# Pooled projections of the token mixer: three rounded passes through the weight ring, most of them early, in place of full-precision products

## The reference, cut to what matters

```python
def token_mixer(h, mix_w_in, conv_w, ..., pool_w, pool_scale, pool_proj, dn_proj, mix_w_out):
    proj = h @ mix_w_in
    xp, q, k, v, z, b_raw, a_raw, g_pool, g_dn = jnp.split(proj, MIX_IN_SPLITS, axis=-1)

    pooled = multiscale_pool(xp)
    ya = jnp.einsum('btgc,gcd->btgd', pooled, pool_w).reshape(B, T, POOL_WIDTH) * pool_scale
    ya = ya @ pool_proj

    qkv = jax.nn.silu(causal_depthwise_conv(jnp.concatenate([q, k, v], axis=-1), conv_w))
    ...
    merged = jax.nn.sigmoid(g_pool) * ya + jax.nn.sigmoid(g_dn) * yb
    return merged @ mix_w_out
```

## Time and profile before

| | |
|---|---|
| runs, median (lowest to highest) | 1830.85 us (1830.83 to 1831.58), 3 runs |
| the profiled execution, first to last instruction | 1829.4 us |
| TensorE busy | 1804.5 us of it |
| mixer, heads of k, q and v | some 985 to 1240 us of the span |

### The profile page before, as it was taken

The page is one execution under the profiler, slowest core; times in us unless marked ns, Lnnn a source line. Parts: engine busy times, 40 slices in busy tenths (PEclk is TensorE's granted clock), DMA queues, the critical chain, the costliest instruction groups (busy, mean ns, idle before and its releaser), DMA issues.

```text
span 1829.4 us, 22015 instructions
## 1 busy us (share of the span) xinstructions
PE 1804.5 (99%) x8636; PEld 1442.0 (79%) x8636; DVE 1090.7 (60%) x1927; ACT 842.3 (46%) x1371; POOL 141.0 (8%) x159
## 2 busy tenths in 40 slices
PE   8999999999999999999999999999999999999998
PEld 6777777767888788888886877788888878888887
DVE  6787888877526887633348777745434763333323
ACT  5777777777423422322225766335422443222221
POOL 2200000000011022100100120100000100000010
PEclk9999999999999999999999999999999999999999
DMA  5422332322243498623323222310222422222231
GB/s 192 138 104 81 116 104 73 113 93 100 73 173 137 163 322 294 212 90 97 100 84 144 78 85 91 104 59 12 81 92 89 153 85 100 95 101 90 95 97 65
DMA packets 59478, 209.21 MB, mean 114 GB/s; under 512 B 6704, under 2 KB 9136, under 8 KB 58736
## 3 DMA queue, kind: packets, MB, share of 16 engines
q1 hardware_dynamic: 47248, 164.54, 26.0%
q0 software_dynamic: 12128, 43.26, 7.1%
HBM read 202.53 MB, written 5.25 MB: 114 GB/s over the span
## 4 chain that ended last, share of the span: by engine, by line
PE 91%; DVE 5%; ACT 2%; issue 1%; DMA 0%; SPq 0%; DVEq 0%; ACTq 0%
PE ps L1335 25%; PE ps L1338 25%; PE ps L1336 24%; PE ps L1424 2%; PE ps L1448 2%; PE ps L1385 2%; PE ps L1386 2%; PE ps L1477 1%; PE ps L1392 1%; DVE wL L1637 1%; ACT wH L2082 1%; PE ps L1436 1%; PE ps L1413 1%; PE ps L1414 1%; DVE affn L1732 0%
## 5 line engine op out<-in xcount | busy, mean ns | idle before, releaser
L1637 DVE TENSOR_TENSOR wL<-wr,wH 128x1024 fp32r<-128x1024 f32 (+1 forms) x297 | 360.0, 1214 | 368.2 <-ACT wH L2082 367.7
L1335 PE MATMUL ps<-hH,wH 128*128 128x512 f32 (+1 forms) x1448 | 577.6, 399 | 1.0 <-DVE hL L1737 1.0
L1338 PE MATMUL ps<-hH,wL 128*128 128x512 f32 (+1 forms) x1448 | 565.4, 390 | 1.0 <-DVE wL L1637 0.7
L1336 PE MATMUL ps<-hL,wH 128*128 128x512 f32 (+1 forms) x1448 | 563.9, 389 | 0.0
L2082 ACT ACTIVATE wH<-wr 128x1024 fp32r<-128x1024 f32 (+1 forms) x297 | 307.6, 1038 | 238.4 <-PE ps L1338 221.3
L1335 PEld LDWEIGHTS ps<-hH,wH 128*128 128x128 f32 (+1 forms) x1448 | 271.3, 187 | 71.1 <-issue 13.1
L1338 PEld LDWEIGHTS ps<-hH,wL 128*128 128x128 f32 (+1 forms) x1448 | 271.0, 187 | 61.9 <-DVE wL L1637 4.0
L1336 PEld LDWEIGHTS ps<-hL,wH 128*128 128x128 f32 (+1 forms) x1448 | 271.4, 187 | 55.9 <-issue 2.6
L1335 PE MATMUL ps<-gffn,wH 128*128 128x512 f32 (+1 forms) x374 | 142.3, 380 | 0.3 <-DVE xT L1875 0.2
L1338 PE MATMUL ps<-gffn,wL 128*128 128x512 f32 (+1 forms) x374 | 140.9, 377 | 0.0
L1336 PE MATMUL ps<-gffn,wH 128*128 128x512 f32 (+1 forms) x374 | 140.9, 377 | 0.0
(11 more groups left out here) (339 smaller groups left out, 2375.3 us busy)
## 6 DMA issues: line engine op xcount, KB each, us to landing
wr<-wst SPq DMA_DIRECT2D x280, 512.0 KB, 3.4
fed<-wfd POOLq DMA_DIRECT2D x56, 512.0 KB, 5.1
xT<-wfd POOLq DMA_DIRECT2D x16, 512.0 KB, 4.0
wr<-wst SPq DMA_DIRECT2D x16, 384.0 KB, 3.0
xT<-xin SPq DMA_DIRECT2D x8, 256.0 KB, 7.3
xT<-xin SPq DMA_DIRECT2D x2, 1024.0 KB, 5.9
xsave<-xT SPq DMA_DIRECT2D x1, 2048.0 KB, 7.2
c<-wfd POOLq DMA_DIRECT2D x8, 256.0 KB, 3.3
```

Source lines behind the costliest of these rows:

```text
L1335: e.matmul(o, hi, vh, start=k == 0, stop=False)
L1336: e.matmul(o, hi, vl, start=False, stop=False)
L1338: i = e.matmul(o, lo, vh, start=False, stop=k == t.nk - 1)
L1637: e.tensor_tensor(dst, x, hi.bitcast(F32), ALU.subtract).then_inc(s[name], 1)
```

## The change

The f32 products go away. `pool_mid` now gives high and low parts of `ya` (`yH`, `yL`, held in the arena `a3r`): ScalarE writes the scaled high part, and VectorE a new low part. `pool_out(c)` becomes a product tile of kind `po` in the ring: four blocks of 128 (a slot of 128 x 512), 12 rounded matmuls in 4 ticks, ScalarE copies the result to `X`. `pool_gate(c)` is the gate tile, after which VectorE multiplies `X` in place. The first `po` tile stands behind the first group of k, ahead of its session's sums; the other seven stand behind the second group of k, and the sessions of q move by 24 and 20 ticks. The eight f32 weight loads leave GpSimd's queue, and SyncE's queue loads eight more slots. The high part of the squares moves to another place in SBUF (`o3r` for `xr`).

```diff
         def pool_mid(g):
-            add("pool_mid", g=g, bank=wk.take()[1], pm=sig("pm"), ya=sig("ya"), pd=g + 1)
+            add("pool_mid", g=g, bank=wk.take()[1], pm=sig("pm"), ya=sig("ya"), yl=sig("yl"), pd=g + 1)
...
         def pool_out(c):
+
+            po = sig("po")
+            yield from self.steps_of(Tile("po", src("pool_proj_2", 128 * c, 4), pb.take()[1], "y", ("po", po), c=c, po=po))
+
+        def pool_gate(c):
             gps = sig("gps")
-            yield from self.steps_of(tile("gp", 4624 + 128 * c, ("gps", gps), c=c, gps=gps))
-            bank, pp, m1 = pb.take()[1], sig("pp"), sig("m1")
-            for k in range(4):
-                add("pool_out", c=c, k=k, bank=bank, pp=pp, m1=m1, gps=gps)
-                yield k
+            yield from self.steps_of(tile("gp", 4624 + 128 * c, ("gps", gps), c=c, gps=gps, po=c + 1, m1=sig("m1")))
...
         session(32, "k", range(4))
         session(76, "k", range(4, 8))
-        session(120, "q", range(4))
-        session(164, "q", range(4, 8))
+        session(144, "q", range(4))
+        session(184, "q", range(4, 8))
...
-        po = iter(range(8))
         for which in "kq":
             for g in range(2):
                 for h in range(4 * g, 4 * g + 4):
                     run(conv(which, h))
-                run(pool_out(next(po)))
+                run(pool_gate("kq".index(which) * 2 + g))
+                if which == "k":
+                    for c in ((0,), range(1, 8))[g]:
+                        run(pool_out(c))
         for h in range(DNH):
             run(conv("v", h))
             if h % 2:
-                run(pool_out(next(po)))
+                run(pool_gate(4 + h // 2))
...
-                    i = e.matmul(ps[d["bank"]][:], b4(pool_buf[c % 2], k), yab[k], start=k == 0, stop=k == 3)
...
+                elif what == "pool_mid":
+                    g = d["g"]
+                    w.wait_ge(s["ya"], d["ya"])
+                    e.scalar_tensor_tensor(yL[g], ps[d["bank"]][:], S("pool_scale", g, g + 1), yH[g].bitcast(F32),
+                                           ALU.mult, ALU.subtract).then_inc(s["yl"], 1)
+                elif what == "out_gp":
+                    v = X[d["c"]]
+                    w.wait_ge(s["po"], d["po"])
+                    w.wait_ge(s["gps"], d["gps"])
+                    e.scalar_tensor_tensor(v, gpb, 1.0, v, ALU.add, ALU.mult).then_inc(s["m1"], 1)
...
-                    e.activation(yab[g], ps[d["bank"]][:], ACT.Copy, scale=S("pool_scale", g, g + 1)).then_inc(s["ya"], 1)
+                    e.activation(yH[g], ps[d["bank"]][:], ACT.Copy, scale=S("pool_scale", g, g + 1)).then_inc(s["ya"], 1)
+                elif what == "out_po":
+                    t = d["t"]
+                    w.wait_ge(s["slot"], t.done)
+                    w.wait_ge(s["saved"], 16)
+                    e.activation(X[d["c"]], ps[t.bank][:], ACT.Copy).then_inc(s["po"], 1)
```

More of the change, by code:

```diff
@@ L868, in session @@
             for j, h in enumerate(hs):
-                at(end + 13 + j + (2 if end == 164 else 0), l2_sum, h, l2s)
+                at(end + 13 + j + (2 if end == 184 else 0), l2_sum, h, l2s)
                 if which == "k":
@@ L874, in session @@
                     at(end + 38 + 2 * j, prep_q, h)
-            at(end + 17 + (2 if end == 164 else 0), l2, which, l2s)
+            at(end + 17 + (2 if end == 184 else 0), l2, which, l2s)
             at(end + 26, l2_end, which, l2s)
@@ L950, in mixer @@
         head_ends()
-        add("mix_out", om=self.count["om"], pp=8, m1=8)
+        add("mix_out", om=self.count["om"], m1=8)
         def zd_out(h):
@@ L1002, in model_kernel @@
     place, n_main = {}, 0
+    proj_at = {one: 1024 * 9216 + 128 * 128 * 4 + 65536 * c for c, one in enumerate(POOLW[4:])}
     for one in slots:
-        if one not in place:
+        if one not in place and one not in proj_at:
             place[one] = n_main
@@ L1023, in several @@
                 return [self(n) for _ in range(k)]
-        with ExitStack() as early:
-            xR = Arena(early, "xr", 4096, F32R)
         xT = alloc(ctx, "xT", 4096)
@@ L1070, in model_kernel @@
         G = Arena(P1a, "g1a", 3072, F32R)
-        sq3_hi = [xR.t[:, 512 * j:512 * j + 512] for j in range(4, 8)]
         sq_hi, sq_lo = G.several(3), G.several(3)
@@ L1103, in model_kernel @@
             F.close()
+        with ExitStack() as early:
+            o3R = Arena(early, "o3r", 8192, F32R)
+        sq3_hi = [o3R.t[:, 6144 + 512 * j:6656 + 512 * j] for j in range(4)]
         M = ExitStack()
@@ L1120, in model_kernel @@
         sq3_lo = [mR.t[:, 14336 + 512 * j:14848 + 512 * j] for j in range(4)]
+        yH, yL = ([mR.t[:, a + 512 * j:a + 512 + 512 * j] for j in range(4)] for a in (2048, 4096))
         Kdr, rB, vB, gpb = [W[:, 0:512], W[:, 512:1024]], yab[0:2], yab[2:4], C("dist")
@@ L1138, in model_kernel @@
         dsol = nc.dram_tensor("dsol", (4 * 65536,), F32, kind="Internal").ap()
-        rhs = {"h": ([c5(hH, c) for c in range(8)], [c5(hL, c) for c in range(8)]), "g": (gH, gL), "o": (oH, oL), "m": (mH, mL)}
+        rhs = {"h": ([c5(hH, c) for c in range(8)], [c5(hL, c) for c in range(8)]), "g": (gH, gL), "o": (oH, oL), "m": (mH, mL),
+               "y": (yH, yL)}
         g_order = [h for z in range(6) for h in (6 + z, z)] + list(range(12, HEADS))
@@ L1252, in weights @@
                 n = slots[j][2] * slots[j][4]
+                src_d, at = (wfd, proj_at[slots[j]]) if slots[j] in proj_at else (wst, place[slots[j]])
                 e.dma_start(wr[:, (j % NRAW) * SLOT:(j % NRAW) * SLOT + n],
-                            wst[place[slots[j]]:place[slots[j]] + 128 * n].rearrange("(p c) -> p c", p=128)).then_inc(s_raw[j % NRAW], 16)
+                            src_d[at:at + 128 * n].rearrange("(p c) -> p c", p=128)).then_inc(s_raw[j % NRAW], 16)
             for c in range(8):
@@ L1314, in ready @@
                     w.wait_ge(s["ol"], k + 1)
+                elif t.rhs == "y":
+                    w.wait_ge(s["yl"], k + 1)
                 else:
@@ L1937, in _ @@
                     e.tensor_scalar(ngc, gc, -1.0, None, ALU.mult, ALU.bypass).then_inc(s["bd"], 1)
[L1938 to L1941, removed]
-                        w.wait_ge(s["saved"], 16)
-                        e.scalar_tensor_tensor(X[d["c"]], gpb, 1.0, ps[d["bank"]][:], ALU.add, ALU.mult).then_inc(s["m1"], 1)
+                elif what == "pool_mid":
[8 more added lines that the diff above has]
+                    e.scalar_tensor_tensor(v, gpb, 1.0, v, ALU.add, ALU.mult).then_inc(s["m1"], 1)
                 elif what == "conv_taps":
@@ L2405, in pool_feed @@
             def pool_feed():
-                if pool_n[0] < len(POOLW):
+                if pool_n[0] < 4:
                     feed(POOLW, pool_buf, s_pool, pool_n[0], pool_at[0])
-                    pool_at[0] += 128 * POOLW[pool_n[0]][2] * 128
+                    pool_at[0] += 128 * 128
                     pool_n[0] += 1
```

21 lines of the change are left out of this document (4 added, 17 removed).

## The result

| | before | after |
|---|---|---|
| runs, median (lowest to highest) | 1830.84 us (1830.18 to 1831.58), 4 runs | 1841.22 us (1840.40 to 1842.73), 4 runs |
| the profiled execution, first to last instruction | 1829.4 us | 1838.5 us |

The ratio is 1.0057, its 95% interval 1.0046 to 1.0069: the change costs 10.4 us. The forecast was 1835.5 us with a range up to 1839.5, so it was slower, as forecast, and by more than twice as much.

What follows compares the result with a forecast made beforehand. TensorE, busy 1804.5 of 1829.4 us, was taken as the bound. A 5.9 us gain against waits of 3.3, 0.4, 4.6 and 2.3 gave +4.7: 1834.1 profiled, 1835.5 us as median, 8-in-10 range 1831.5 to 1839.5.

Steps and rivals of the forecast that it cites:

- The gain: Eight f32 product groups, 27.5 us, become 96 rounded passes at 0.225 us, 21.6 us: 5.9 us less.
- Place 1: Sums of the first group of k: TensorE waits for VectorE's low part behind copy, gate multiplication and split: +3.3 us.
- The +0.4: Late weight split for the slot behind the first short po tile, in the first group of k: +0.4 us (0 to 0.9).
- Place 2: Sums of the second group of q: more VectorE work before head 7's low part; +4.6 us, a wait of about 5.9.
- Place 3: End of v: without the f32 group TensorE stands until head 7's silu ends, before the transposes: +2.3 us.
- The rival that VectorE has caught up: Seven tiles let VectorE reach q's head 7 early, so no wait there: 1829.6 us, half caught up 1832.5; chance 0.23.
- The sum: Gain and added waits together: -5.9 + 3.3 + 0.4 + 4.6 + 2.3 = +4.7 us.
- the step that took the clock for a rival: Clock falls to 1.2 GHz in the long wait at Place 2, 14 slow passes, 3 us more: 1838.5 us; chance 0.15.
- The rest of the program unchanged within 0.5 us: Sign to check: attention and feed-forward, outside the changed places, stay as they were within 0.5 us.
- The base: Starting time: the profiled 1829.4 us, plus 1.45 us by which the median of the runs lies above it.

Runs made afterwards that it cites:

- the tile of double length: Kernel after the change with 12 unneeded passes in front of each po tile, 96 in all: 1858.56 us.
- all three waits filled: Kernel after the change with passes whose result is overwritten ahead of its three long TensorE waits (12, 22 and 8): 1836.44 us.
- the kernels with filled waits: Kernel after the change with unneeded TensorE passes ahead of Place 2 alone, Places 2 and 3, or all three: 1838.3, 1837.8, 1836.44 us.
- the four kernels that carry unneeded passes: Kernel after the change with passes ahead of one, two or three waits, or before each po tile: 1838.3, 1837.8, 1836.44, 1858.56 us.
- the version with the gate tiles moved: Kernel after the change, gate multiplication 6 ticks later, no gate tile behind k's second group, two at the end, q's last sums 3 ticks later: 1831.16 us.

## Why the prediction was wrong

**The gain, -5.9 us: right in kind, 0.6 too large.** In a `po` tile of the profile after, six passes from one row to the other:

```profile
1061.80 0.39 PE L1347 MATMUL ps<-a3r,wL 128*128 128x512 f32 x1
...
1063.16 0.39 PE L1347 MATMUL ps<-a3r,wL 128*128 128x512 f32 x1
```

That is 0.227 for a pass, 21.8 us for 96. Summed from the starts of all 96 passes it is 22.2, since some steps between tiles are longer, so the gain is 5.3.

**Place 1, +3.3: right, in its parts too. The +0.4: the right size at another place.** The wait is 3.02 us. The queue costs 4.26 less 2.03, 2.2 (forecast 2.3). VectorE comes 1.7 later (1.8): its last tap ends 0.49 us later in the trace although this execution began 1.19 earlier. The forecast laid 0.4 on the slot behind the first short tile, at place 1; no wait is there, and the 0.47 that the trace has is behind the run of seven (1080.64).

**Place 2, +4.6, a wait of 5.9: right.** The wait is 5.68, which is 4.4 more than the earlier trace rows: 3.75 in VectorE's queue (forecast 3.9) and 0.65 because TensorE comes sooner (0.7).

**Place 3, +2.3: right.** The wait is 2.15.

**The rival that VectorE has caught up: false,** as the tile of double length shows most plainly.

**The sum, +4.7: the mixer without any fall of the clock is 5.25 us longer.** The measured terms, -5.3 + 3.0 + 0.5 + 4.4 + 2.15, add up to 4.7 again: a gain taken too large and waits taken too large cancel, which is luck. The other 0.5 us of the 5.25 is assigned to nothing. With all three waits filled the program takes 1836.4 us, 0.9 over the 1835.5 of the forecast: its mechanism and sizes held but for the clock.

**What failed is the step that took the clock for a rival and gave it 0.15.** The forecast said against it that the wait of the earlier trace rows comes "before any steady work, and the wait at place 2 is behind 100 us of it". Steady work in front did not protect it. Over the traces of all kernels with their waits left open, the clock fell behind place 2 every time that the wait was 3.0 to 5.7 us (eight of eight; not behind 2.1 or 1.3 us), behind place 1's wait of 3.0 us in three of seven, and behind place 3's 2.15 us in four of six. The fall also was priced at one place, while all three waits can have it: 2.9 us for two, 5.3 for three, in place of 3 for one. Sum and falls belonged together as the forecast, at 1838 to 1841. Of the 5.7 us between forecast and result, 2.9 are this step in the profiled execution. The rule that an idle array goes back to 1.2 GHz, which the prediction quoted from the Trainium skill's "TensorE: Matmul & The Clock Gate", section "What's actually happening", was thus the better guide than my reason against it.

**"The rest of the program unchanged within 0.5 us" failed too.** From behind the recurrence to the second feed-forward the changed kernel is 2.0 and 1.7 us longer. 0.4 of it is there in the kernels with filled waits too: one more weight split is waited for. The remainder is the wait for `xT`, 1.8 us, behind a weight load that ScalarE waited for 8.1 us in the profile after, and 6.2 before. It was 0.2 us in both profiles of before and in the four kernels that carry unneeded passes, and 0.9 to 1.8 in the other eight profiles. The two go together: ScalarE waited 6.0 to 6.3 us for that load in the first six profiles and 7.2 to 8.1 in the eight. So the load came late; what makes it late I did not find. It is no matter of the clock, since the version with the gate tiles moved has it without a fall. It is no chance of one execution either, as I had expected of the second profiles: both profiles of before have 0.2, both of after 1.8 and 1.5. Its cause stays open.

**The base.** The profiled execution before started 1.3 us later than its second profile, but that is no error of the forecast: 1829.4 and the 1.45 us added to it are the median of the runs, 1830.85.

The account, from the first pass on: 5.25 for the mixer, 2.9 for the clock, 2.0 and 0.15 behind it are 10.3 us, against 10.4 between the medians of the runs.

## What to carry to other kernels

Work that fills TensorE costs its duration; a wait costs its duration and what the clock then takes, here some 1.3 to 2.7 us for each fall at the three places. No safe length of a wait came out of these traces: 2.1 us at place 2 brought no fall, 2.15 at place 3 brought it in four of six, and at the inverse's small products it fell behind 1.1 and 1.5 us. So a change that trades TensorE work for waits is to be priced with the fall at each new wait, not with one fall as an unlikely case. A wait at a sum is set by the few operations queued between its input and its producer; look at that stretch of the queue, since time given to the engine further up does not reach it.

## What the runs showed that was not expected

The same wait, to 0.02 us, brought the clock down in one execution and not in another. Behind it the lower level lasted for 7 passes of 512 columns in one profile at place 2, 1.4 us of loss, and for 12 in another, 2.6 us (1175.56 to 1181.22, 13 passes that take 3.05 at the full clock). The slow stretch itself was about equally long in both; in the first it began 3.7 us before the wait's end, in the second 1.2, and only what lies behind the wait costs. The change as profiled, then the kernel with each tile twice:

```profile
1153.40:1160.20 6.80, 3.11 (x7) 2.49 (x8) 6.59 (x14) 2.38 (x5) 0.00 (x0) 0.50 0.29 87
```

```profile
1174.40:1181.10 6.70, 5.54 (x13) 4.41 (x14) 6.46 (x13) 2.77 (x5) 0.00 (x0) 0.50 0.42 153
```

Passes without use in the waits made the program 4.8 us faster, 2.9 of them by the clock. And a GpSimd operation of 1.5 us on a 128x512 tile held up a VectorE tap of 0.48 us, which took 1.51 and ended behind it.
